# One core, two transformer-like blocks in float32: modulation products in four column strips, loads in another order, and two norms with tokens on the partitions

## The reference, cut to what matters

```
def rms_norm(x, g):
    xf = x.astype(jnp.float32)
    var = jnp.mean(xf * xf, axis=-1, keepdims=True)
    return (xf * lax.rsqrt(var + EPS)).astype(x.dtype) * g

def adaln(cvec, w, b):
    m = jax.nn.silu(cvec) @ w + b
    return jnp.split(m, 3, axis=-1)
...
        sh_l, sc_l, gt_l = adaln(c, ada_w[i], ada_b[i])
        h_lat = rms_norm(x_lat, norm_g[i]) * (1.0 + sc_l[:, None]) + sh_l[:, None]
        if i % N_MIXERS == 0:
            sh_c, sc_c, gt_c = adaln(c_ctx, ada_w[i], ada_b[i])
            h_ctx = rms_norm(x_ctx, norm_g[i]) * (1.0 + sc_c) + sh_c
...
        h = h + FFN_RESIDUAL_WEIGHT * swiglu_ffn(rmsnorm(h, ffn1_norm[l]), ffn1_w_gu[l], ffn1_w_down[l])
        h = h + token_mixer(rmsnorm(h, mix_norm[l]), w_in[l], ...)
```

## Time and profile before

| | |
|---|---|
| median of three runs | 2444.23 us (2442.29 to 2445.59) |
| the profiled execution's own time | 2442.99 us |
| its span | 2441.3 us |
| PE busy | 2382.5 us, 98% of the span |
| PE weight loads busy | 2073.3 us, 85% |
| DVE busy | 1641.4 us, 67% |
| ACT busy | 1036.5 us, 42% |

### The profile page before, as it was taken

How to read it: one execution, slowest core, us unless ns; L and a number is a source line. 1 busy time by engine, 2 the same in 40 slices (tenths; PEclk the granted TensorE clock), 3 DMA queues, 4 the chain that set the end, 5 groups by cost and what they waited for, 6 DMA issues and landing times.

```text
span 2441.3 us, 46321 instructions
## 1 busy us (share of the span) xinstructions
PE 2382.5 (98%) x17214; PEld 2073.3 (85%) x17214; DVE 1641.4 (67%) x2395; ACT 1036.5 (42%) x1418; POOL 111.7 (5%) x138
## 2 busy tenths in 40 slices
PE   7999999999999989999999999989999999999997
PEld 3888888888888867888899999978999778888886
DVE  7578888888888855455564343469999975534446
ACT  4446545554654424333353222245545554322223
POOL 0012111111211100000000000000000000000000
PEclk9999999999999999999999999999999999999999
DMA  6212222222222322222222222223232222232223
GB/s 247 84 64 86 77 77 77 86 69 69 86 77 79 113 104 69 78 79 83 97 86 87 94 87 87 93 81 101 95 101 96 95 86 95 95 98 100 95 95 104
DMA packets 61990, 224.01 MB, mean 92 GB/s; under 512 B 6736, under 2 KB 8784, under 8 KB 61552
## 3 DMA queue, kind: packets, MB, share of 16 engines
q1 hardware_dynamic: 58992, 211.08, 25.8%
q0 software_dynamic: 2944, 12.19, 1.5%
HBM read 221.15 MB, written 2.10 MB: 91 GB/s over the span
## 4 chain that ended last, share of the span: by engine, by line
PE 60%; DVE 4%; ACT 1%; issue 1%; ACTq 0%; DVEq 0%
PE ps L511 59%; ACT w_hi L1128 1%; DVE w_lo L1690 0%; DVE n_tmp L1714 0%; DVE n_sq L1709 0%; DVE hb L2084 0%; DVE n_lo L1717 0%; DVE cv L2507 0%; DVE fin L2572 0%; DVE n_sq L2346 0%; DVE n_sum L1728 0%; DVE y_lo L1717 0%; DVE rt L1969 0%; DVE n_sq L2529 0%; PE ps L842 0%
## 5 line engine op out<-in xcount | busy, mean ns | idle before, releaser
L1128 ACT ACTIVATE w_hi<-w_raw 128x1024 fp32r<-128x1024 f32 (+1 forms) x360 | 377.9, 1050 | 911.5 <-PE ps L511 886.1
L1690 DVE TENSOR_TENSOR w_lo<-w_raw,w_hi 128x1024 fp32r<-128x1024 f32 (+1 forms) x360 | 435.5, 1210 | 215.0 <-ACT w_hi L1128 210.8
L511 PE MATMUL ps<-h_hi,w_hi 128*128 128x512 f32 x640 | 264.2, 413 | 4.3 <-DVE h_lo L1823 2.6
L511 PE MATMUL ps<-h_hi,w_lo 128*128 128x512 f32 x640 | 251.9, 394 | 0.0
L511 PE MATMUL ps<-h_lo,w_hi 128*128 128x512 f32 x640 | 251.6, 393 | 0.0
L511 PE MATMUL ps<-y_lo,w_hi 128*128 128x512 f32 x504 | 178.2, 395 | 7.4 <-DVE y_lo L1717 7.4
L511 PE MATMUL ps<-v_hi,w_hi 128*128 128x512 f32 x416 | 163.0, 392 | 3.4 <-DVE v_lo L2542 2.8
L511 PE MATMUL ps<-n_hi,w_hi 128*128 128x264 f32 (+1 forms) x576 | 155.2, 324 | 9.3 <-DVE n_lo L1717 8.5
L511 PE MATMUL ps<-v_hi,w_lo 128*128 128x512 f32 x416 | 161.9, 389 | 0.0
L511 PE MATMUL ps<-v_lo,w_hi 128*128 128x512 f32 x416 | 161.9, 389 | 0.0
L511 PE MATMUL ps<-n_hi,w_lo 128*128 128x264 f32 (+1 forms) x576 | 155.6, 325 | 0.0
(11 more groups left out here) (384 smaller groups left out, 5341.2 us busy)
## 6 DMA issues: line engine op xcount, KB each, us to landing
w_raw<-in_weights_dram SPq DMA_DIRECT2D x376, 512.0 KB, 3.2
ada_raw<-in_ada_weights_dram SPq DMA_DIRECT2D x4, 2048.0 KB, 20.7
gate_raw<-in_gate_weights_dram POOLq DMA_DIRECT2D x16, 512.0 KB, 3.6
x<-in_x_dram SPq DMA_DIRECT2D x1, 2048.0 KB, 12.4
x<-in_x_dram POOLq DMA_DIRECT2D x1, 2048.0 KB, 8.8
out_dram<-fin SPq DMA_DIRECT2D x16, 128.0 KB, 1.9
xc<-in_ctx_dram SPq DMA_DIRECT2D x1, 1024.0 KB, 19.0
masks<-in_masks_dram POOLq DMA_DIRECT2D x1, 512.0 KB, 5.0
```

Of the source, the lines that this page charges most:

```text
L511: last = nc.tensor.matmul(o, w, xp, start=start and n == 0, stop=stop and n == 2)
L1128: run(w_hi[:, s, 0:n], w_raw[:, s, 0:n], ACT.Copy).then_inc(hi_ready[s], 1)
L1690: tt(w_lo[:, s, 0:n], w_raw[:, s, 0:n], w_hi[:, s, 0:n].bitcast(F32), ALU.subtract).then_inc(lo_ready[s], 1)
```

## The change

Three places are rewritten.

1. Start. Each quarter of the modulation weights is loaded in two halves of 1 MB (a half of the columns of each block, so pieces of 2 KB), and SP's order is x, quarter 0, context, quarter 1, weight block 0, quarter 2, weight block 1, quarter 3. The product of 512 columns becomes four of 128 columns that go to the four 32-column strips of the array (`tile_position`), and leave their two rows at partitions 0, 32, 64 and 96. One copy of 128 columns and one 128x128 transpose for each quarter follow. The squares of the context are summed on PE (eight products). DVE treats the context ahead of the first two cuts. Ahead of quarter 3 PE waits for block 0's cut and runs `keep_warm` products, whose result is not used, there and after the last transpose. Then blocks 0 and 1 are multiplied in turn for each k (`first_blocks`).
2. End of head 0. Part "c" of block 3 comes after block 4, `begin_head(1, ...)` ahead of the transposes of `v_st`, ACT cuts block 6 ahead of the copies of `v_st`, DVE runs `prepare` ahead of the cut of block 7.
3. N1 and NMIX. `norm_by_token` uses the sum and the last square as stationary operands, so that PE leaves one sum a token on the partitions, in 4 columns of 128 tokens (6 of 88 for NMIX). Root and reciprocal run on these few elements; DVE spreads the reciprocals onto diagonals, and one product with `ones_d` brings them to all partitions, in PSUM, from where `norm_apply` reads them. The last `after` of the residual comes behind the root on ACT and behind the diagonals on DVE.

```
-        ADA_LOADS = [(ada_raw[0][:], 0, 4), (ada_raw[1][:, 0:4], 4, 8), (ada_raw[1][:, 4:8], 8, 12),
-                     (ada_raw[1][:, 8:12], 12, 16)]
+        ADA_QUARTERS = (ada_raw[0][:], ada_raw[1][:, 0:4], ada_raw[1][:, 4:8], ada_raw[1][:, 8:12])
+        ADA_ROWS = 32
...
+            sp.dma_start(x0[:], x_in).then_inc(x_in_s, 16)
+            load_ada(0)
+            sp.dma_start(xc[:], ctx_in).then_inc(xc_in_s, 16)
+            load_ada(1)
+            load_first(0)
+            load_ada(2)
+            load_first(1)
+            load_ada(3)
+            with sp.Fori(1, BLOCKS_TO_FT // 2) as i:
...
-            pool.wait_ge(ada_loaded[3], 16)
+            pool.wait_ge(ada_loaded[7], 16)
...
+            def norm_by_token(N, R, n, total, square, spread):
+                w = NORM_TILE[n]
+                at = [slice(t * w, (t + 1) * w) for t in range(n // w)]
+                pe.wait_ge(R["add"], KD + 1)
+                pe.wait_ge(R["res"], KD + 1)
+                for b_, c in zip(TOKEN_BANKS, at):
+                    nc.tensor.matmul(ps[0:w, b_, 0:2], total[:, c], ones_d[:, 0:2], start=True, stop=False)
+                pe.wait_ge(R["sq"], KD + 1)
+                for b_, c in zip(TOKEN_BANKS, at):
+                    last = nc.tensor.matmul(ps[0:w, b_, 0:2], square[:, c], ones_d[:, 0:2], start=False, stop=True)
+                last.then_inc(N["mean"], 1)
+                pe.wait_ge(N["turned"], 1)
+                for dst, diagonal in spread:
+                    last = nc.tensor.matmul(dst, ones_d[0:w], diagonal, start=True, stop=True)
+                last.then_inc(N["spread"], 1)
...
-                for k in range(KD):
-                    if n == 1 and k == KD - 2:
-                        mean(N0, T, st_sum[:, 0])
-                    last = nc.tensor.matmul(ps[0:2, n], csil[:, k], raw_[:, :, k * P:(k + 1) * P],
-                                            start=k == 0, stop=k == KD - 1)
...
+            def keep_warm(n):
+                for _ in range(n):
+                    nc.tensor.matmul(ps[:, 6], w_hi[:, 0, 0:P], w_hi[:, 0, 0:T], start=True, stop=True)
+            def ada_products(n):
+                for half in range(2):
+                    if n == 3:
+                        keep_warm(3 - half)
+                    pe.wait_ge(ada_loaded[2 * n + half], 16)
+                    for k in range(half * (KD // 2), (half + 1) * (KD // 2)):
+                        for q in range(4):
+                            r0 = q * ADA_ROWS
+                            last = nc.tensor.matmul(ps[r0:r0 + 2, n, 0:P], csil[:, k],
+                                                    ADA_QUARTERS[n][:, q, k * P:(k + 1) * P], start=k == 0,
+                                                    stop=k == KD - 1, tile_position=(0, r0))
...
+            ada_products(0)
+            mean(N0, T, st_sum[:, 0])
+            for k in range(KD):
+                pe.wait_ge(R0C["sq"], k + 1)
+                nc.tensor.matmul(ps[:, 5, 0:TC], ones_d[:], st_tmpc[:, k % 2], start=k == 0, stop=k == KD - 1
+                                 ).then_inc(R0C["add"] if k < KD - 1 else N0C["mean"], 1)
+            ada_products(1)
+            ada_products(2)
...
+            for n in range(3):
+                turn_ada(n)
+            pe.wait_ge(lo_ready[0], 2)
+            ada_products(3)
+            turn_ada(3).then_inc(ada_done, 1)
             pe.wait_ge(N0C["root"], 1)
+            keep_warm(5)
...
+            def first_blocks():
+                xs = as_cut(N0, whole(h_hi, h_lo))
+                s = [take(k) for k in range(2)]
+                for k in range(2):
+                    pe.wait_ge(acc_free, 2 * k)
+                for k in range(KD):
+                    for n in range(2):
+                        last = tiles(s[n], [ps[:, n]], xs, [k], k == 0, k == KD - 1, k)
+                        if k == KD - 1 and n == 0:
+                            last.then_inc(w_used[s[n]], 1)
...
+                if j is None:
+                    project(3, "a"); project(3, "b"); project(4, "a"); project(4, "b"); project(3, "c")
+                    project(5, "ada"); begin_head(1, 6, hs); turn_v_next()
+                    return
...
-            mean(N1, T, n1["sum"][:, 0])
+            norm_by_token(N1, RC, T, n1["sum"][:, 0], n1["sq"][:, 0], [(ps[:, 7], n1["tmp"][:, 1])])
...
-            mean(NMIX, TM, n2["sum"][:, 0])
+            norm_by_token(NMIX, RD1, TM, n2["sum"][:, 0], n2["sq"][:, 0],
+                          [(ps[:, 6 + q, 0:HALF], n2["tmp"][0:NORM_TILE[TM], 1, q * HALF:(q + 1) * HALF]) for q in range(2)])
...
+            def turn_by_token(N, n, diagonal):
+                w = NORM_TILE[n]
+                r_ = by_token[0:w, 0:n // w]
                 dve.wait_ge(N["root"], 1)
-                own.link(v.reciprocal(rt_, rt_))
+                own.link(v.reciprocal(r_, r_))
+                stt(diagonal[0:w].rearrange("p (t c) -> p t c", c=w),
+                    ident[0:w, 0:w].unsqueeze(1).broadcast_to([w, n // w, w]), float(D),
+                    r_.unsqueeze(2).broadcast_to([w, n // w, w]), ALU.mult, ALU.mult).then_inc(N["turned"], 1)
...
             over_root(N0, x0, st_sq[:])
+            over_root(N0C, xc, st_tmpc[:, 2])
             cut(0)
             cut(1)
-            over_root(N0C, xc, st_tmpc[:, 2])
...
                         after(4)
+                        prepare()
                         after(5)
-                        prepare()
...
+            turn_by_token(N1, T, n1["tmp"][:, 1])
+            after(3)
+            st.leave(1)
```

More of the change, by code:

```diff
@@ L69 @@
 HALF_TILE = P // 2
+NORM_TILE = {T: P, TM: TM // 6}
+TOKEN_BANKS = (4, 5, 6, 7, 0, 1)
 QUARTER = P // 4
@@ L573, in _ @@
-            pe.wait_ge(ident_in_s, 16)
[L574 to L578, removed]
+            def keep_warm(n):
+                for _ in range(n):
+                    nc.tensor.matmul(ps[:, 6], w_hi[:, 0, 0:P], w_hi[:, 0, 0:T], start=True, stop=True)
+            def ada_products(n):
+                for half in range(2):
+                    if n == 3:
[7 more added lines that the diff above has]
+                                                    stop=k == KD - 1, tile_position=(0, r0))
+                last.then_inc(ada_part, 1)
@@ L1341, in act_head @@
                 early_after(5)
-                refill(4)
+                if j is not None:
+                    refill(4)
                 stage(4)
@@ L1364, in _, with residual, one @@
             act_head(None, None, HEADS - 1)
-            def residual(R, trips, nb, src, sq, sums, ahead=True, done=0, square_first=True):
-                def one(i):
+            def residual(R, trips, nb, src, sq, sums, ahead=True, done=0, square_first=True, closing=False):
+                def one(i, last=False):
                     for a in range(2):
@@ L1371, in one @@
                         for q in range(nb):
+                            if last and a and q == nb - 1:
+                                fetch_root()
                             if sums and square_first and q == nb - 1:
                                 square_one(R, m_, src(m_), sq, 2)
-                            after(a * nb + q)
+                            if not (last and a and q == nb - 1):
+                                after(a * nb + q)
                         if sums and not square_first:
                             square_one(R, m_, src(m_), sq, 2)
-                if ahead:
+                if closing:
+                    with hinted(act, 0, trips - 1) as i:
+                        st.enter(i, 2 * nb)
+                        one(i)
+                    st.leave(trips - 1)
+                    st.enter(0, 2 * nb)
+                    one(trips - 1, True)
+                elif ahead:
                     with hinted(act, 0, trips) as i:
@@ L1506, in block_norm @@
             def block_norm(N):
-                fetch_root()
-                act.wait_ge(N["sum"], 1)
-                root(N, ps[:, 6:8, 0:HALF], halves(n2["sq"][:, 0]))
+                root_by_token(N, TM)
+                after(1)
+                st.leave(1)
                 norm_hi(N, lambda k: n_hi[:, k, 0:TM], lambda k: n2["tmp"][:, k % 2], lambda k: zero[:])
@@ L1538, in feed_forward @@
                              lambda m_: row(hb, m_)[:, c0:TM], n2["sq"][:, 0, 0:n], final,
-                             not (final and last) or tag in half_done, square_first=tag not in half_done)
+                             not (final and last) or tag in half_done, square_first=tag not in half_done,
+                             closing=final and not last)
             def half_square(R, n, a, half):
@@ L2084, in one @@
                         stt(r_, acc, factor(m_), r_, ALU.mult, ALU.add).then_inc(R["res"], 1)
-                        if last and a:
-                            close_sums(R, N, *sums)
-                        if cuts:
+                        if cuts and not (last and a):
                             after(a * nb + nb - 1)
```

105 lines of the change are left out of this document (59 added, 46 removed).

## The result

The changed kernel takes **2454.96 us** (median of 5 runs, 2452.55 to 2455.39), where the kernel before takes 2444.23: ratio 1.004, 95% interval 1.0029 to 1.0051. It is slower by 10.7 us (0.4%); 2432.5 was forecast, with a range of 2427 to 2439. The profiled execution has a span of 2452.6 us, against 2441.3.

What follows compares the result with a forecast made beforehand. TensorE was taken as the bound, by its waits and small work between back-to-back passes. Gains of 3.7+1.4+1.7+4.4 = 11.2 us gave 2431.8 from the profiled 2443.0, 2433.0 from the median; 2432.5 was said, range 2427 to 2439.

Steps and rivals of the forecast that it cites:

- The step that failed: Whole program: TensorE's 512-column passes run at 0.228 us between its waits, so time taken off a wait reaches the end.
- rival 3: Start: the column strips take turns, TensorE stays the bound, first block 8.7 to 14.9 late, 2444 to 2450 us; 5%.
- The same step, second half: Inside the stream of weight blocks: a microsecond taken off an engine other than TensorE does not reach the end.
- Rival 4: Start: its gain meets another wait and the change does little, within 0.2%; 3%.
- Start: Start to first weight block: first pass at 42.6 (41.0 to 44.7) against 46.30, 3.7 us gained (1.6 to 5.3).
- rival 1: Lower clock all through and slow load pieces: all lower ends, 6.7 us gained, 2436.3; 22%.
- rival 2: The clock holds from 34 on: quarter 3 ends at 37.8, all upper ends, 14.8 us gained, 2428.2; 18%.
- First two blocks: Weight blocks 0 and 1, interleaved per operand: 1.4 us gained (0.5 to 2.0), third block 15.4 after the first.
- End of head 0: End of head 0: block 3's context part covers block 6's cut, v_st is late next; 1.7 us gained (0.7 to 2.5).
- Norms: N1 and NMIX: narrow products, root and reciprocal shorten the chain from square to n_tmp; 4.4 us for both (3.9 to 5.0).
- the spread: At both norms, the product bringing reciprocals to all partitions: taken as 1.25 us, 0.7 more at half clock.
- The sum: All places together: 3.7+1.4+1.7+4.4 = 11.2 us gained, ends 6.7 and 14.8.

Runs made afterwards that it cites:

- e5: The whole change with by_token in a slot freed by eps and zero, so operands keep the addresses of before: 2437.35 us, ratio 0.9968 to before.
- e2: The kernel before with only an unused tensor of 32 bytes a partition where the change takes by_token: 2465.90 us, ratio 1.0084.
- e12: The kernel before with the new start alone, old head 0 and old norms, operands at old addresses: 2443.75 us, ratio 0.9996.
- e4: The kernel before with the new start and new head 0, old norms, without by_token: 2438.22 us, ratio 0.9973.
- e10: The kernel before with the new form of the two norms alone, operands at old addresses: 2441.06 us, ratio 0.9984.
- e17: e5 with both e16's passes on constants at the norms and e13's cut memset: 2431.05 us, ratio 0.9942 to before.
- e1: The changed kernel with by_token made 64 bytes a partition instead of 32: 2443.27 us, ratio 0.9992 to before.
- e11: e5 with VectorE's small memset at the start cut in 2 pieces: 2438.87 us, ratio 0.997 to before.
- e14: e5 with VectorE's small memset at the start cut in 32 pieces: 2436.51 us, ratio 0.9965 to before.
- e13: e5 with VectorE's small memset at the start cut in 16 pieces: 2435.52 us, ratio 0.9964 to before.
- e16: e5 with unread 512-column passes on constants put into TensorE's waits at the two norms: 2433.64 us, ratio 0.9958 to before.

## Why the prediction was wrong

The mechanisms of the three rewritten places were right, and the sum was made on a ground that the change itself moved.

- **The step that failed** is the first: "between such places TensorE runs passes of 512 columns back to back, 0.228 us each. So a microsecond taken off a place where TensorE waits ... reaches the end". I took the pace of the untouched passes as given: I costed every instruction that the change adds and put its memory at nothing. The 32 bytes of `by_token` made the last stage's passes 0.233 instead of 0.226 us, 17.6 us in sum (changed kernel against e5; e2 gives 21 on before). None of the rivals held this; rival 3, the one on the slow side, stood for another cause.
- **The same step, second half.** The start's gain did not reach the end either: e12 was 5.2 us ahead at the last head and 0.8 behind at `g_lo`, and some 5.6 of that went in VectorE's gap and the lower clock behind it. "One taken off another engine inside the stream does not" count was wrong too: VectorE's 3 us did count. Rival 4 (the gain meets another wait) had this at 3%.
- **Start.** 42.6 (41.0 to 44.7) forecast, 41.48 to 42.5 measured, passes at 0.033 (0.027 taken). Half quarters took 1.89 us from 11.79, 14.39 and 34.37 (granted clock 0.50 from 34 to 37) and 1.05 from 29.85 and 37.29; the granted clock was 1.00 from 38 on, and for the first weight block, 41.48 to 45.70. So neither rival 1 (the lower clock all through) nor rival 2 (full clock from 34 on) came true at the start, though the first block begins as early as rival 2 has it. Warming passes stand ahead of both, and no run leaves them out, so that they held the clock is not shown. The last products ended at 38.34, against 39.4; the last half was in by 37.29 (36.9 forecast). (The upper end of 40.9 does not follow from its terms, which give 41.3; the range goes by 41.5.)
- **First two blocks.** 15.4 forecast, 14.8 measured (third block at 56.24), 2.0 gained instead of 1.4, with the slow passes already in; here too the full clock stands behind it. **End of head 0:** 1.05 idle for `v_st` at 79.98, as argued. Together the new head 0 brought 4.2 at the first `y_lo` (e4 at 793.6, e12 at 797.8), against 1.4+1.7.
- **Norms.** 4.4 forecast, 3.4 measured (e10). The chain was right; what was too small is the spread, taken at 1.25 us, with 0.7 more at half clock as the bad case. In e10 both spreads ran at a granted clock of 0.50, 2.08 and 2.13 us, and `n_tmp` began 4.5 and 5.0 us after the square instead of 6.2 and 6.6: 1.7 and 1.5 gained, 3.2 of the 3.4. The 2.2 came only where the spread ran faster: N1 in e5 (1.56 us) and NMIX in the changed kernel (1.41).
- **The sum** at the old addresses is 7.8 us (e5), against 11.2. e17, without the gap and with the clock held at the norms, has 14.3; the passes that hold the clock were no part of the forecast, so this does not bear it out.

## What to carry to other kernels

Before you cost what a change executes, look at what it allocates: list the addresses of all operands of the long streams of passes before and after, and keep their distance to the weights. If a stretch nobody edited changes its count of passes in a window at the same clock, suspect the layout, and test it with an unused tensor, not with the change. And follow a gain at the start through the program: here it ended at an engine that, as far as the traces tell, had run out of instructions.

## What the runs showed of the hardware

- The pace of 512-column passes depends on the distance between stationary and moving operand: 0.226 us where it is a multiple of 256 bytes (as before, and 256 more), 0.229 at 64 bytes past one, 0.233 at 32, 128, 192 and 224 past one. Passes of 256 columns came out the other way: in head 0 they start 0.120 us apart before and in e5, 0.117 in e2 and the changed kernel.
- VectorE stood still for 2.2 to 3.5 us in the middle of its program with nothing to wait for, while the queue of instructions moved a packet as a weight block ended; where it does so moves with the length of its program.
- Passes that share their rows and go to four column strips ran 0.033 us apart at 128 columns at full clock (32 in 1.05 us).
- Not settled: TensorE has a gap of 2.4 to 2.6 us with nothing to wait for near 1450 in e1, e5, e11 and e14, and not in the changed kernel, e13, e16 and e17. The changed kernel and e5 have the same instructions there. Each of these is one execution, and the executions of one kernel differ by more than the gap (e14 2429.2 to 2438.6 us, e5 2433.5 to 2439.5), so it may come and go within a kernel. It could be a fetch too, but no run was made on it.
